# Two-layer diffusion step on one core: the next pair's first projections in a pair's tail, and an inversion on four quadrants of TensorE

## The reference

```python
h = rmsnorm(x, norm_mix_pre) * (1.0 + sc1) + sh1     # sc1, sh1 from silu(c) @ ada_w + ada_b
z = h @ w_in                                         # 512 channels each of r, k, v; q, k, v; q, k, v, g; gates
z_rwkv = dwconv3(z[..., :o0], rwkv_conv)             # three taps along the tokens
# branch a, 8 heads of 64, two directions:  S = S * w_t + (S a_t) b_t^T + v_t k_t^T ;  y_t = S r_t
out_a = (groupnorm(y) * ln_g + ln_b + bonus) * g @ w_o_rwkv
out_b = softmax attention of q, k, v @ w_o_na        # context and a neighbourhood of the grid
out_c = (groupnorm(retention(q, k, v)) * ret_gn) * silu(g) @ w_o_ret
merged = gates[:, :, 0] * out_a + gates[:, :, 1] * out_b + gates[:, :, 2] * out_c
x = x + g1 * rmsnorm(merged @ w_out, norm_mix_post)
x = x + g2 * rmsnorm(conv_ffn(h2, ffn_up, ffn_conv, ffn_down), norm_ffn_post)
```

## Time and profile before

| | |
|---|---|
| median of 3 runs | 2025.21 us (2020.05 to 2028.73) |
| profiled execution | 2030.75 us, span 2028.6 us |
| PE busy | 1905.9 us, 94% of the span |
| PEld busy | 1718.9 us |
| DVE, ACT, POOL busy | 1001.8, 939.8, 944.0 us |
| granted clock of TensorE, mean | 0.982 of 2.4 GHz |

### The profile page before, as it was taken

One profiled execution on the slowest core, in us unless ns is written; L12 is line 12 of the kernel. 1 busy time (PEld: TensorE's weight loads), 2 busy tenths in 40 slices (PEclk: granted clock), 3 DMA queues, 4 the chain that ended last, 5 costly groups with the idle time before them and its releaser, 6 DMA issues.

```text
span 2028.6 us, 41739 instructions
## 1 busy us (share of the span) xinstructions
PE 1905.9 (94%) x17940; PEld 1718.9 (85%) x17940; DVE 1001.8 (49%) x1516; ACT 939.8 (46%) x1766; POOL 944.0 (47%) x767
## 2 busy tenths in 40 slices
PE   6899999999999989999988999999999998999997
PEld 2887878797899879999947878787879997899996
DVE  2574747475611255552057657475745133555502
ACT  4554645454533454443345555364554334544432
POOL 1434426170666626666416153342516664466663
PEclk9999999999999989999989999999999999999998
DMA  7314232232443314434453141413224432244442
GB/s 291 101 50 143 64 117 94 89 115 86 135 124 122 120 63 124 124 122 127 123 204 124 50 140 55 136 65 125 87 88 156 125 125 83 94 125 125 125 125 73
DMA packets 65414, 231.52 MB, mean 114 GB/s; under 512 B 7376, under 2 KB 11856, under 8 KB 64592
## 3 DMA queue, kind: packets, MB, share of 16 engines
q1 hardware_dynamic: 59040, 215.21, 33.3%
q10 hardware_dynamic: 6192, 13.66, 1.9%
HBM read 223.58 MB, written 5.26 MB: 113 GB/s over the span
## 4 chain that ended last, share of the span: by engine, by line
PE 79%; DVE 9%; ACT 4%; issue 3%; POOL 2%; DMA 2%; ACTq 1%; SPq 0%; DVEq 0%; POOLq 0%
PE psz L471 57%; PE psw L471 20%; DVE work L1360 3%; ACT work L954 3%; DMA ring<-in_w 2%; POOL ringlo L1735 1%; DVE work L1369 1%; PE psz L479 1%; PE psw L479 1%; ACT whi L954 1%; DVE rstd L1369 1%; DVE part L1360 1%; DVE work L1363 1%; POOL work L1771 1%; DVE work L1366 0%
## 5 line engine op out<-in xcount | busy, mean ns | idle before, releaser
L1735 POOL TENSOR_TENSOR ringlo<-ring,whi 128x512 fp32r<-128x512 f32 x608 | 811.1, 1357 | 756.7 <-ACT whi L954 756.7
L471 PE MATMUL psz<-hhi,whi 128*128 128x386 f32 x1696 | 587.1, 346 | 23.2 <-POOL ringlo L1735 14.5
L471 PE MATMUL psz<-hlo,whi 128*128 128x386 f32 x1696 | 577.6, 341 | 0.0
L471 PE MATMUL psz<-hhi,ringlo 128*128 128x386 f32 x1696 | 576.4, 340 | 0.0
L954 ACT ACTIVATE whi<-ring 128x1024 fp32r<-128x1024 f32 x304 | 320.2, 1053 | 133.4 <-PE psz L471 125.1
L471 PE MATMUL psw<-work 64*64 64x64 f32 (+4 forms) x9024 | 348.8, 232 | 17.6 <-issue 9.1
L471 PEld LDWEIGHTS psw<-work 64*64 64x64 f32 (+2 forms) x9024 | 294.5, 137 | 73.1 <-issue 55.6
L471 PEld LDWEIGHTS psz<-hhi,whi 128*128 128x128 f32 x1696 | 321.0, 189 | 36.1 <-issue 18.9
L471 PE MATMUL psz<-part,whi 128*128 128x386 f32 x1344 | 346.6, 339 | 3.2 <-DVE work L1360 1.5
L471 PEld LDWEIGHTS psz<-hlo,whi 128*128 128x128 f32 x1696 | 322.9, 190 | 2.1
L471 PEld LDWEIGHTS psz<-hhi,ringlo 128*128 128x128 f32 x1696 | 321.0, 189 | 0.0
(11 more groups left out here) (107 smaller groups left out, 1725.2 us busy)
## 6 DMA issues: line engine op xcount, KB each, us to landing
ring<-in_w SPq DMA_DIRECT2D x400, 512.0 KB, 3.5
pk<-in_pk ACTq DMA_DIRECT2D x8, 832.0 KB, 4.4
const<-in_const SPq DMA_DIRECT2D x1, 1795.0 KB, 10.0
work<-in_x SPq DMA_DIRECT2D x1, 1544.0 KB, 6.8
work<-in_x ACTq DMA_DIRECT2D x1, 1544.0 KB, 6.5
out_x<-work ACTq DMA_DIRECT2D x1, 1544.0 KB, 5.5
work<-out_x ACTq DMA_DIRECT2D x1, 1544.0 KB, 9.8
out_x<-work SPq DMA_DIRECT2D x4, 386.0 KB, 2.3
```

The costliest lines, as they stand in the source:

```text
L471: ins = nc.tensor.matmul(out, a, b, start=start, stop=stop, skip_group_check=True)
L1735: L.do(G.tensor_tensor(out, a, b, op), S[sig] if sig else None)
```

## The change

**The layer's head.** Each block of `ada_w` is used by four matmuls of 256 columns into four column groups of the array, where it was two of 512 into two; the blocks' contents are laid out anew for it. The sum of squares is taken in one piece, ahead of block 6 (block 10 in the second layer), where its eight matmuls were strewn between the blocks. ACT copies the four rows after the last block.

```diff
-for jp in range(2):
-  for k in range(KT):
-    b = ADA0 + KT * jp + k
-    loaded(b)
-    for i in range(2):
-      j = 2 * jp + i
-      mm(psw[32 * j:32 * j + 2, 1, :], cs[:, k, :], ring2[b % RING][:, i, :], k == 0,
-       k == KT - 1, "row_done" if k == KT - 1 else None)
-    used[0] += 1
-    i = b - ADA0 - (KT if layer else KT // 2)
-    if 0 <= i < KT:
-      sum_squares(0, (i,))
+for b in range(2 * KT):
+  if b == (10 if layer else 6):
+    sum_squares(0)
+  jp, k = divmod(b, KT)
+  loaded(b)
+  for j in range(4):
+    mm(psw[32 * j:32 * j + 2, 1, 256 * jp:256 * jp + 256], cs[:, k, :],
+     ring2[b % RING][:, j // 2, 256 * (j % 2):256 * (j % 2) + 256], k == 0, k == KT - 1,
+     "row_done" if b == 2 * KT - 1 else None)
+  used[0] += 1
 pe.wait_ge(*after("row_ready", 4))
```

```diff
+  ahead = [0]
+  def next_steps(n):
+    if p + 1 == PAIRS:
+      return
+    for _ in range(n):
+      i, k = divmod(ahead[0], KT)
+      zi, j = zb + ZI["r"] + i, bb + 10 + i
+      if k == 0:
+        opened(zi)
+        pe.wait_ge(*after("w_lo", 2 * j + 2))
+      three(z(zi), j, k, hsp[k], k == 0, k == KT - 1, "z_done" if k == KT - 1 else None)
+      ahead[0] += 1
...
+  if p == 0:
+    for i in (1, 2):
+      dense(ZP + i, bb + i)
+    dense(zb + ZI["nq"], bb + 3)
+    dense(zb + ZI["nk"], bb + 4)
+    key_sums()
+    pe.wait_ge(*after("lora_in", 2))
+    lora_up()
+  else:
+    key_sums()
+    dense(zb + ZI["nq"], bb + 3)
     pe.wait_ge(*at_of("yroot_ready", p - 1, 0))
     pe.wait_ge(*at_of("rroot_ready", p - 1, 0))
-  pe.wait_ge(*at_of("kk_sq", p, 0))
-  mm(w(0), blk, tb, sig="kkn_done")
-  pe.wait_ge(*at_of("kk_rk", p, 0))
-  mm(w(1), blk, kd, sig="bon_done")
+    lora_up()
+    dense(zb + ZI["nk"], bb + 4)
+  dense(zb + ZI["nv"], bb + 5)
+  dense(zb + ZI["rq"], bb + 6)
   pe.wait_ge(*after("pk_in", 16 * (p + 1)))
-  pe.wait_ge(*after("lora_in", 2))
-  lora = pk[:, PK["lora"]:PK["lora"] + 256]
-  for d in range(2):
-    mm(w(2 + d), lora[0:64, d * P:(d + 1) * P], lwal[0:64, :], sig="lw_done")
...
   attend(0)
-  dense(zb + 9, bb + 7)
-  dense(zb + 10, bb + 8, between=lambda: attend(1))
-  dense(zb + 11, bb + 9, between=lambda: attend(2))
-  turned(zb + 12, zb + 10, mixed[2][p])
-  values_mm(0)
+  dense(zb + ZI["rv"], bb + 8)
+  dense(zb + ZI["rg"], bb + 9, between=lambda: attend(1))
+  turned(zb + ZI["rvt"], zb + ZI["rv"], mixed[2][p])
+  mm(opened(zb + ZI["g"]), pk[:, PK["g_up"]:PK["g_up"] + P], lgl, sig="z_done")
+  attend(2)
```

```diff
-      pe.wait_ge(*at_of("x_ready", p, 0 if lv == 1 else 2 * (lv - 2) + hb + 1))
-      for x in range(6):
+    pe.wait_ge(*at_of("x_ready", p, 0 if lv == 1 else 2 * (lv - 2) + 2))
+    for x in range(6):
+      for hb in range(2):
         for c in range(2):
-          mm(psw[hc(c), g_bank(lv, hb), CH * x:CH * x + CH], au[hc(c), hb, x, 0, 0:CH],
+          mm(psw[hc(c ^ hb), g_bank(lv, hb), CH * x:CH * x + CH], au[hc(c), hb, x, 0, 0:CH],
...
+      ada_steps(3 if lv == 4 else 4)
...
-          mm(psw[hc(c), x_bank(lv, hb), CH * x:CH * x + CH], a_[hc(c), hb, x, :],
-           b_[hc(c), hb, x, :], sig="xt_done" if (x, c) == (5, 1) else None)
+          e = c ^ hb
+          o_ = psw[hc(e if lv == LEVELS - 1 else c), x_bank(lv, hb), CH * x:CH * x + CH]
+          mm(o_, a_[hc(e), hb, x, :], b_[hc(e), hb, x, :],
+           sig="xt_done" if (x, c) == (5, 1) else None)
     if lv <= 4:
       values_mm(lv + 1)
     if lv == 4:
-      ada_steps(2)
+      ada_steps(3)
       keys_flipped()
...
+    elif lv == LEVELS - 1:
+      ada_steps(4)
```

```diff
+def across():
+  for c in range(2):
+    flip(tvv[hc(1 - c), 1:2], xv[hc(c), 1:2], "tv_ready" if c else None)
...
+    L.do(V.tensor_tensor_scan(Ls[:, order], rst[:, order], sg[d][:, order], 0.0, ALU.mult, ALU.add),
+      S["scan_ready"])
+    if p:
+      (scale_rwkv, scale_ret)[d](p - 1)
+    if d:
+      attend(0)
+      if p:
+        finish_ret(p - 1)
+    dve.wait_ge(*after("sig_ready", 4 * p + d + 3))
+    L.settle()
+    tt(tb, kk, aa[d])
+    dve.wait_ge(*after("kd_ready", 2 * p + d + 1))
+    tt(kd, kd, kc_)
+    L.settle()
+    dve.wait_ge(*after("exp_ready", 6 * p + 3 * d + 3))
+    stt(ar[:, d, 0, :], kk, -1.0, Px)
+    tt(bk[:, d, 1, :], kd, Pi)
+    tt(bk[:, d, 0, :], tb, Pi, sig="til_ready")
+  attend(1)
+  if p:
+    finish_rwkv(p - 1)
+  dve.wait_ge(*after("bon_done", p + 1))
+  tt(bonus, w(1), vc, sig="bon_used")
+  attend(2)
...
     if lv < 4:
...
       pred(by_dir(xv[:, hb]), level_mask(lv, 0), by_dir_of(x_bank(lv, hb)), "x_ready")
     if lv < LEVELS - 1:
       L.settle()
-      flip(tvv, xv, "tv_ready")
+      flip(tvv[:, 0:1], xv[:, 0:1])
+      across()
```

```diff
     run(gg.rearrange("p h x c -> p h (x c)"), psw[:, b:b + 2, 0:384], sig="gl_ready")
     if lv <= 4:
       attend(lv + 3)
+    else:
+      split(sb_ + 10)
     if lv == 1:
...
+  late_rows(p, zb + ZI["ada"])
+  split(sb_ + 11)
   for c in range(2):
...
       run(nst[:, e::2, d, :], w(2 + c, 192 * d, 192).rearrange("p (i v) -> p i v", i=3), sig="nn_ready")
+  split(sb_ + 12)
...
-  split(sb_ + 10)
+  def next_tap(i):
+    if p + 1 < PAIRS:
+      centre_tap((rc, kc_, vc)[i], zb + ZI["r"] + i, "conv", 4 * i + p + 1)
+      split(sb_ + 13 + i)
+  next_tap(0)
   retain(4)
...
+  next_tap(1)
...
-  split(sb_ + 11)
...
-  split(sb_ + 12)
   if p + 1 < PAIRS:
     load_pack(p + 1)
+  next_tap(2)
```

More of the change, by code:

```diff
@@ L48 @@
 PAIR0 = SHARED0 + 2
-PAIR_BLOCKS = 10 + 8
+PAIR_BLOCKS = 7 + 8 + 3
 MERGE0 = PAIR0 + PAIR_BLOCKS * PAIRS
@@ L551, in keep_warm, with sum_squares @@
                             mm(w(3, 0, 256), ones, const[:, 0:256])
-                    def sum_squares(j, tiles=range(KT)):
-                        for k in tiles:
+                    def sum_squares(j):
+                        for k in range(KT):
                             pe.wait_ge(*after("sq_ready", KT * j + k + 1))
@@ L1060, in _ @@
                                 act.wait_ge(S["x_st"].h, 16)
-                        if p:
-                            act.wait_ge(*at_of("til_ready", p - 1, 1))
-                            act.wait_ge(*at_of("rr_ready", p - 1, 1))
-                        for i, dst in enumerate((rc, kc_, vc)):
-                            centre_tap(dst, zb + i, "conv", 4 * i + p)
-                            split(sb_ + i + 3)
-                        seen(zb + 3)
-                        run(nq, z(zb + 3), free=zb + 3, scale=0.125)
@@ L1080, in _, with query_in @@
-                        act.wait_ge(*at_of("kkn_done", p, 0))
-                        run(Pi, w(0), ACT.Sqrt, "kkn_root")
+                        if p == 0:
+                            for i, dst in enumerate((rc, kc_, vc)):
+                                centre_tap(dst, ZP + i, "conv", 4 * i)
+                                split(sb_ + i + 3)
+                        def query_in():
+                            seen(zb + ZI["nq"])
+                            run(nq, z(zb + ZI["nq"]), free=zb + ZI["nq"], scale=0.125)
+                            split(sb_ + 6)
@@ new lines, in key_in, with key_root @@
+                        def key_in():
+                            seen(zb + ZI["nk"])
+                            if p:
+                                act.wait_ge(*after("out_k", 32 * p))
+                            run(nk, z(zb + ZI["nk"]), free=zb + ZI["nk"])
+                            L.settle()
+                            act.dma_start(nak[layer, p], nk[:, 0:P]).then_inc(S["out_k"].h, 16)
+                            split(sb_ + 7)
+                        def key_root():
+                            act.wait_ge(*at_of("kkn_done", p, 0))
+                            run(Px, w(0), ACT.Sqrt, "kkn_root")
```

288 lines of the change are left out of this document (154 added, 134 removed).

## The result

| | before | after |
|---|---|---|
| median, 7 runs each | 2025.21 us | 2036.66 us (2030.85 to 2040.89) |
| ratio | | 1.006, 95% interval 1.004 to 1.008 |
| profiled execution, span | 2028.6 us | 2038.9 us |
| granted clock, mean | 0.982 | 0.965 |

The forecast was 1968 us, with a range of 1932 to 2003. The change made the kernel 0.6% slower, and the forecast misses by 68.7 us. In the profiled executions the first layer takes 424.6 us from its first scan to the merge's first product, where it took 418.5 before; the second takes 421.3, where it took 415.2. The forecast had 24.9 less than before in each, so about 62 of the 68.7 us lie in the pairs.

A forecast was written before the change was run, and what follows sets the result against it. TensorE, busy 94% of the span, was taken to bound the kernel. Savings of 39.7 us in six pair steps, 10 in the fourth pairs and 8 in the layers' heads, 57.7 in all, gave 1968 us, range 1932 to 2003.

The forecast's parts named there:

- 28.2 us of levels before: Inversion levels 1 to 5 of the third pair before the change: 11.9 for levels 1 and 2, 16.3 for 3 to 5.
- A set of 24 on four quadrants at 0.76 us: Inversion products: 24 products, 48 instructions, fall from 1.61 us on two quadrants to 0.76 on four.
- The rival of the shared bank: Inversion products: a shared bank, not the quadrants, sets 33.5 ns, so nothing speeds up; 2010 us, chance 0.10.
- VectorE sets the levels: Inversion: VectorE's work mostly sets the new levels' pace; 12.15 us for levels 1 and 2, 17.5 for 3 to 5.
- The rival of levels at TensorE's pace: Inversion: VectorE does not set the levels, which fall to about 25 us; 1931 us, chance 0.15.
- Level 1 at 7.2 us: Inversion level 1: crossing transposes stand ahead of job 3's maximum, with ACT's exponential and copy to `gg` behind it; 7.2 us.
- 0.5 us for the first step's weights: Tail's start: 0.5 us set for the first step's weights, as ACT splits block r in level 5 once landed.
- The rival's 2040: Dry ring: block r's late load holds ACT, `wm` and the tail about 9 us a pair; 2040 us, chance 0.05.
- The head at 0, the gate's stall at 1.8 in place of stalls that go: Pair's head: `g` waits some 1.8 us for its bank, replacing stalls of about that sum; net 0, head 45.1 us.
- 4 us in each layer's head: Layers' heads: sum in one piece and four-column-group matmuls save 4 us each (between 0 and 6), 8 in all.
- The steps fill the gaps: Tail: the next pair's 24 projection steps fill TensorE's gaps of 3.7 us; tail 30.2 us, 7.0 saved.
- The rival that they fill nothing: Tail: steps push the ACT and DVE chain on, 3.7 us of gaps stay in six tails; 1990 us, chance 0.13.

The follow-up runs named there:

- e4: Changed kernel with ScalarE's copy of job 1's values and level 1's copy to gg moved ahead of job 3's exponential: 2011.2 us, ratio 0.9940.
- e8: e1 with e4's move on ScalarE, so the old two-quadrant inversion in the changed kernel: 2027.1 us, ratio 1.0003.
- e1: Changed kernel with the inversion of the kernel before (two quadrants, heads staggered), keeping the changed ada steps: 2027.6 us, ratio 1.0014.
- e14: Changed kernel with e7's ada steps (3 behind level 3, 7 in level 4, 6 in level 5), level 1 as it is: 2013.1 us.
- e7: e4 with the 16 ada steps earlier: 3 in level 3, 7 in level 4, 6 in level 5, none in the tail: 1995.8 us.
- e9: e7 with two of the 16 ada steps moved back from level 5 to the tail: 1993.8 us, ratio 0.9862.
- e13: Changed kernel with one move on TensorE, attention job 2 ahead of the gate's product: 2030.1 us, ratio 1.0021.
- e12: e10 with TensorE's attention job 2 ahead of the gate's product, which waits for Silu: 1980.3 us, ratio 0.9795.
- e5: e4 with the layers' heads of the kernel before (512-column products, strewn sum of squares, old layout): 2009.3 us, ratio 0.9925.
- e11: e7 with the next pair's r, k, v steps in three pieces of 8 behind the state chain, not eight pieces of 2 to 4: 2064.0 us.
- e10: e7 with VectorE's finish of branch a and the bonus ahead of attention job 0's maximum: 1995.7 us, ratio 0.9869.
- e16: e12 with e9's ada steps, old layers' heads, the gate's product further back, and ScalarE's copies for job 2 ahead of Silu: 1976.6 us.
- e6: e4 with TensorE's job 2 at once, the gate behind job 3, and VectorE's finish of branch a ahead of job 1: 2026.9 us.

## Why the prediction was wrong, step by step

- *TensorE bounds, and time is won where its list shrinks.* Half right. Its busy time fell by 38 us, and none of that reached the end.
- *28.2 us of levels before.* A slip of my sum. These 28.2 us start at the end of the first transposes, and the new levels, 29.65 by my own list, start at the end of the COPY_PREDICATED ahead of them. Counted in that way the levels before took 29.24, so by my own figures the inversion loses 0.4 a pair and not 1.4, and the forecast would have been 1960, further off. The 1.0 us of difference went into my head of 57.9.
- *A set of 24 on four quadrants at 0.76 us.* Right in kind: 0.93 us busy, 0.86 from start to next start at 379.46. The rival of the shared bank, at 1.61, is dead. The Trainium skill, TensorEngine Tiling (Array Packing), Restrictions and Gotchas, says that different row tiles cannot access one PSUM bank at the same time. Here both halves of the rows wrote each bank, each to its own half of the bank's partitions, and the set did not go back to 1.61. What the 0.10 us above my 0.76 are is open.
- *VectorE sets the levels.* Right for levels 2 to 4, and in level 5 it waits 1.89 for TensorE's four ada steps and `xt`, as I had it: from 365.68 on they took 5.2, 5.4, 5.9 and 6.2 us against 4.95, 5.4, 6.0 and 6.1. With level 1 mended, level 2 is 4.84. Two of my sizes were wrong and cancelled, which is luck: the three transposes took 1.79 us against 1.55, and the two COPY_PREDICATED, no longer staggered, 1.05 against 1.25. The rival of levels at TensorE's pace is dead too.
- *Level 1 at 7.2 us.* **The first step that failed.** It took 8.9 to 10.5. I had the exponential behind the crossing transposes and the copy to `gg` behind it, but not ScalarE's copy of job 1's values between them, for which TensorE's next transposes wait; so `xt` came later than I had it, and at 1.2 GHz. e4 gives 7.08 for one moved line, and 25 us; e8 and e1 show that the line matters only with the new inversion.
- *0.5 us for the first step's weights.* **The second.** The tail ran from 388.37 to about 421.7, 33.3 us against my 30.2. I had the mechanism as a rival and put its threshold at a landing of 8 us. Four to five were enough: the load is issued only when ada block 3 is used, in level 5, so ScalarE waited until 389.61. My argument against it, that half of the DMA engines' time is free, was read in another stretch; from 389 to 390 us their share was 1.04. I had asked when the whole chain breaks, not what each us of wait costs when ScalarE's copies of `wm` stand behind it and the clock falls. The rival's 2040 is near the time measured, but by another sum. e14 prices it at 23.6 us alone, e7 at 15.4 behind e4; e9 shows that it is not the number of steps in the tail.
- *The head at 0, the gate's stall at 1.8 in place of stalls that go.* **The third.** The wait was named and sized well (1.50 and what lies around it), but job 2 stands behind it, and with it the masks. In the third pair what is left of the step beside levels and tail was 45.2 us against 45.1; the 1.0 us of the slip above hides a loss of that size. e13: 6.5 us alone; e12: 15 once VectorE is out of the way.
- *4 us in each layer's head.* Failed by its size: e5 shows nothing clear of the noise, where 8 us would have shown. My own argument, that the sum lasts as long as five loads, was right and spoke against the gain: a full ring stops, and TensorE waits for it afterwards (2.74 and 2.02).
- *The steps fill the gaps.* Held: in the third pair's tail TensorE has no wait behind the first step (from 394 to 422 us). With e7 a step is 105.5 us, with e12 103.4, against 104.9. e11 shows what the tail is with the steps in three pieces. The rival that they fill nothing is dead.
- *No stretch at 1.2 GHz.* Wrong: the mean clock fell to 0.965. Behind the waits in level 1 and at the tail's start TensorE ran at 1.2 GHz, so that these cost more than their length.

In the third pair the step missed its 104.9 by 5.2 us: 2.0 in the levels (31.6 against 29.65), 3.1 in the tail, 0.1 in the rest.

The sum: 2036.7, less 25.4 (e4), 15.4 (e7) and 15.5 (e10 and e12 together), is 1980.3. Of the 12 us left to the forecast, 8 are the layers' heads; e16 is 4 below e12. So a pair as short as the forecast's is what this work allows, not what this order gives. What stays open: why e12's move is worth 15 with e10 and 6.5 alone, and the price of one cut row of steps. Level 1's stall did not swallow the rest: e13's levels take 257.5 us in all, 2 less than the changed kernel's. A part of it is the head: from a pair's first scan to its first COPY_PREDICATED (its end), 36.3 us in the changed kernel, e13 takes 35.6 and e12 35.0. e12's edit without e10's was not run on e4 or e7.

## What to carry to other kernels

When an instruction gets longer on one engine, go down the lists of the others: list every instruction that stands behind the one that waits for it, in program order, and ask of each who waits for it. All three misses were unrelated work standing behind a wait: two copies on ScalarE, and on TensorE an attention job. A prefetch is timed from the release of its slot; give each us of its lateness a price, and take it as a rival from the first us, not from where everything breaks. Work that releases a slot was best put into the earliest idle time here, level 3, and not into the nearest (e7, e9 and e14).

## What was new of the hardware

- STREAM_TRANSPOSE went by columns and not by partitions in these shapes: three of 384 columns, two of them on 64 partitions only, took 1.79 us (370.88), and one on 64 partitions 0.57 (e6's trace), where 768 columns on 128 took 0.98.
- Products on four quadrants whose two row halves write the same bank, each to its own half of the partitions, are not put one behind the other: 48 instructions over two banks took 0.86 us to the next start, 17.9 ns each, against 33.5 on two quadrants and 15.8 in the loop of the earlier trace rows.
- After TensorE had waited 2.10 us (level 1) or 1.42 us (the tail), among short matmuls, it ran at 1.2 GHz (granted clock 0.50), and in e12's fourth pair after waits of 0.46 and 0.94, but not in its third after the same: 1.56 us for 48 instructions and not 0.93, 0.32 us a dense matmul and not 0.18. A window of 10 us in the second pair's tail has a granted clock of 0.66:

```profile
280.00:290.00 10.00, 8.43 (x179) 7.40 (x173) 1.33 (x3) 5.02 (x12) 4.23 (x4) 0.66 0.19 59
```
